# Recurrent solve: two queries of a key in one product, state and query products joined beside copied keys

## The reference, cut to what matters

```
def step(state, inp):
    r_t, w_t, k_t, v_t, a_t, b_t = inp
    sa = einsum('bhij,bhj->bhi', state, a_t)
    state = state * w_t + sa[..., None] * b_t + v_t[..., None] * k_t
    y_t = einsum('bhij,bhj->bhi', state, r_t)
```

## Time and profile before

| | |
|---|---|
| median of 3 runs | 1055.91 us (1055.52 to 1057.32) |
| span of the profiled execution | 1055.6 us |
| PE busy | 1014.7 us (96%), 8574 matmuls |
| DVE busy | 534.4 us (51%) |
| ACT busy | 312.3 us (30%) |
| the recurrent solve | from 199.4 to 319.9 us, 11% of the span |
| mean granted TensorE clock | 0.995 of full |
| HBM read | 272.06 MB |

### The profile page before, as it was taken

One profiled execution on the slowest core, in us unless ns is written; L12 is line 12 of the kernel. 1 busy time (PEld: TensorE's weight loads), 2 busy tenths in 40 slices (PEclk: granted clock), 3 DMA queues, 4 the chain that ended last, 5 costly groups with the idle time before them and its releaser, 6 DMA issues.

```text
span 1055.6 us, 19485 instructions
## 1 busy us (share of the span) xinstructions
PE 1014.7 (96%) x8574; PEld 659.2 (62%) x8574; DVE 534.4 (51%) x815; ACT 312.3 (30%) x536; POOL 131.4 (12%) x152
## 2 busy tenths in 40 slices
PE   8999999999898989999999999999999999999998
PEld 6777899998895678778788443344444443444343
DVE  4568842255546876575665433344333333433354
ACT  4467742033236751231333121111111111111110
POOL 0000000374974500000000100000000000000000
PEclk9999999999999999999999999999999999999999
DMA  9632021000004057466488899999999999999994
GB/s 389 236 116 112 3 81 43 12 5 5 4 4 161 2 186 270 135 224 227 187 368 330 327 409 419 426 427 427 426 427 427 427 425 427 426 428 418 415 415 161
DMA packets 42981, 273.34 MB, mean 259 GB/s; under 512 B 8032, under 2 KB 8176, under 8 KB 28688
## 3 DMA queue, kind: packets, MB, share of 16 engines
q1 hardware_dynamic: 39488, 264.42, 62.1%
q0 software_dynamic: 2400, 4.28, 1.2%
q10 hardware_dynamic: 1008, 3.38, 0.9%
HBM read 272.06 MB, written 4.19 MB: 262 GB/s over the span
## 4 chain that ended last, share of the span: by engine, by line
PE 82%; DMA 8%; DVE 6%; ACT 2%; issue 1%; SPq 0%; DVEq 0%; POOLq 0%; ACTq 0%
PE banks L1722 29%; PE banks L2251 18%; PE banks L2265 9%; DMA w_qkv<-in_w 4%; DMA w_tok<-in_w 4%; PE banks L2289 2%; PE banks L1881 2%; PE banks L2290 2%; PE banks L2257 2%; PE banks L1883 2%; PE banks L1896 1%; PE banks L2237 1%; ACT xT L929 1%; DVE ring L1342 1%; PE banks L1946 1%
## 5 line engine op out<-in xcount | busy, mean ns | idle before, releaser
L1601 DVE TENSOR_TENSOR hid<-banks,silu_a 64x512 f32<-64x512 f32 x32 | 22.2, 693 | 197.9 <-ACT silu_a L934 197.9
L2265 PE MATMUL banks<-w_ring,hidT 128*64 128x512 f32 x512 | 116.8, 598 | 1.1 <-ACT hidT L938 1.1
L1588 DVE SCALAR_TENSOR_TENSOR mod<-banks,row_weight,mod 64x512 f32<-64x512 f32 x64 | 47.9, 748 | 70.3 <-PE banks L2265 69.3
L2251 PE MATMUL banks<-w_tok,xT 128*64 128x512 f32 x176 | 78.3, 596 | 1.8 <-DMA w_ring<-in_w 1.8
L934 ACT ACTIVATE silu_a<-banks 64x512 f32<-64x512 f32 x32 | 18.9, 591 | 206.4 <-PE banks L2252 206.4
L2252 PE MATMUL banks<-w_tok,xT 128*64 128x512 f32 x176 | 79.6, 606 | 0.0
L2252 PE MATMUL banks<-w_ring,xT 128*64 128x512 f32 x176 | 78.3, 596 | 0.0
L1595 DVE TENSOR_TENSOR x<-x,banks 128x1024 f32<-128x1024 f32 x60 | 71.8, 1219 | 12.6 <-PE banks L2290 12.2
L2265 PEld LDWEIGHTS banks<-w_ring,hidT 128*64 128x64 f32 x512 | 34.3, 136 | 67.0 <-issue 65.7
L2251 PE MATMUL banks<-w_ab,xT 128*64 128x512 f32 x160 | 72.4, 606 | 3.8 <-DMA w_tok<-in_w 3.8
L1722 PE MATMUL banks<-x_r,ring_r 128*128 128x512 f32 x192 | 74.8, 390 | 0.0
(11 more groups left out here) (392 smaller groups left out, 2301.6 us busy)
## 6 DMA issues: line engine op xcount, KB each, us to landing
w_ring<-in_w SPq DMA_DIRECT2D x42, 2048.0 KB, 25.5
w_tok<-in_w SPq DMA_DIRECT2D x16, 2048.0 KB, 26.2
ada_buf<-in_w_ada SPq DMA_DIRECT2D x64, 256.0 KB, 3.6
w_ab<-in_w SPq DMA_DIRECT2D x8, 2048.0 KB, 25.9
w_qkv<-in_w SPq DMA_DIRECT2D x7, 2048.0 KB, 29.6
w_tok<-in_w SPq DMA_DIRECT2D x24, 512.0 KB, 16.6
w_ring<-in_w SPq DMA_DIRECT2D x24, 512.0 KB, 17.1
w_ring<-in_w SPq DMA_DIRECT2D x10, 1024.0 KB, 14.6
```

The source lines that it names most:

```text
L1588: dve.scalar_tensor_tensor(dst[:, 512 * n:512 * n + 512], bank[5][SLOTS * n:SLOTS * n + SLOTS, :], weight_of(e), gate2[:, n, :], ALU.mult, ...
L1601: dve.tensor_tensor(hid[:, :], bank[3][SLOTS:P, :], silu_a[:, :], ALU.mult).then_inc(hid_v, 1)
L2251: pe.matmul(bank[2][0:SLOTS, :], rows, w1_of(k), start=(k == 0), stop=(k == KT - 1))
L2265: mm = pe.matmul(bank[5][SLOTS * n:SLOTS * n + SLOTS, :], hidT[:, k, :], w2[:, k, 512 * n:512 * n + 512], start=(k == 0), stop=(k == 3))
```

## The change

- `zr` and `ahat` become two parts of one buffer, so that the two queries of a token, 14 tiles apart, can be read by one product. The addresses stay the same.
- `forms` makes one product of 128 columns per key (the `a` query and the `r` query) where it made two of 64. The order of the forms in `FORMS[k]` turns round: (b, r), (k, r), (b, a), (k, a). The mask follows it.
- `FORMS[k]` gets a fifth form, `BT`: a copy of the keys `Bt`, made by ACT (`end_keys`, one of 128x256 per group and half, before its "x" copies). The group's other buffers move up by 256 floats.
- "gh" multiplies `w_` by (b, r) and by the copied keys in one product of 128 columns. The event "q" on PE is gone, and with it its waits; the query part now lies in the left half of `a_`, the state part in the right half. `queries_added` waits for "gh".

The core of the diff:

```diff
-        FORMS = [flat[:, 3072 * k:3072 * k + 1024].rearrange("p (f h n) -> p f h n", f=4, h=4) for k in range(NG)]
+        FORMS = [flat[:, 3072 * k:3072 * k + 1280].rearrange("p (f h n) -> p f h n", f=5, h=4) for k in range(NG)]
+        RB, KR, TT_, AK, BT = range(5)
...
-        MM_EVENTS = ["ab", "t0", "x"] + LEVELS + ["wu", "gh", "q"]
+        MM_EVENTS = ["ab", "t0", "x"] + LEVELS + ["wu", "gh"]
...
+            def end_keys(half, k):
+                sc, g = 2 * half + k // 2, k % 2
+                act.activation(FORMS[k][:, BT, :, :].rearrange("p (j o) n -> p j o n", o=2),
+                               tokm[:, sc, 2 * g:2 * g + 2, 1, :].rearrange("p j (o n) -> p j o n", o=2), ACT.Copy).then_inc(solve_a[k], 1)
+
+            act.wait_ge(turn_a, TT * CT)
             for half in range(2):
-                for ev in A_EVENTS:
+                for k in range(NG):
+                    end_keys(half, k)
+                for ev in A_EVENTS[1:]:
...
             def queries_added(half, k):
-                dve.wait_ge(solve_mm[k], mm_at(half, "q"))
+                dve.wait_ge(solve_mm[k], mm_at(half, "gh"))
...
-                    for f in range(4):
+                    for f in range(2):
                         for odd, c in ((0, 0), (1, 1), (0, 1), (1, 0)):
-                            key = (bhat[rows, ct, toks], zr[rows, 4 + ct, toks])[f % 2]
-                            query = (ahat[rows, ct, toks], zr[rows, ct, toks])[f // 2]
-                            mm = pe.matmul(bank[2 * k + odd][CH * c:CH * c + CH, P * f + CH * j:P * f + CH * j + CH], key, query, start=True, stop=True)
+                            key = (bhat[rows, ct, toks], zr[rows, 4 + ct, toks])[f]
+                            onto = bank[2 * k + odd][CH * c:CH * c + CH, :].rearrange("p (q f n) -> p q f n", q=2, f=2)[:, :, f, CH * j:CH * j + CH]
+                            mm = pe.matmul(onto, key, zr_all[rows, ct:ct + 15:14, toks], start=True, stop=True)
...
-                        elif ev == "gh":
-                            mm = pe.matmul(a_[rows, at], w_, Bt, start=True, stop=True)
                         else:
-                            mm = pe.matmul(a_[rows, 256 + CH * i:256 + CH * i + CH], w_, rb, start=True, stop=True)
+                            pe.matmul(a_[rows, :].rearrange("p (q h n) -> p q h n", q=2, h=4)[:, :, i, :], w_, FORMS[k][rows, RB:BT + 1:BT, i, :], start=True, stop=True)
...
-                        elif ev == "gh":
-                            pe.wait_ge(solve_a[k], a_at(half, "wu"))
                         else:
-                            pe.wait_ge(solve_v[k], v_at(half, "g"))
+                            pe.wait_ge(solve_a[k], a_at(half, "wu"))
```

More of the change, by code:

```diff
@@ L46, in shape_constants @@
              "before": (r < c) * 1.0,
-             "causal2": np.concatenate([r % CH < np.arange(CH)[None, :], r % CH <= np.arange(CH)[None, :]], 1) * 1.0}
+             "causal2": np.concatenate([r % CH <= np.arange(CH)[None, :], r % CH < np.arange(CH)[None, :]], 1) * 1.0}
     row, col = r % CH, np.arange(CH)[None, :]
@@ L130, in hybrid_layer @@
         hT = sb("hT", [P, KT, SEQ])
-        zr = sb("zr", [P, 14, SEQ])
-        ahat = sb("ahat", [P, CT, SEQ])
+        zr_all = sb("zr", [P, 14 + CT, SEQ])
+        zr, ahat = zr_all[:, 0:14, :], zr_all[:, 14:14 + CT, :]
         bhat = sb("bhat", [P, CT, SEQ])
@@ L765, in _ @@
                         else:
[L766 removed]
+                            src, dst = a_[:, :], group_part(k, 1280, 512, 8)
                         act.activation(dst.rearrange("p h n -> p (h n)"), src, ACT.Copy).then_inc(solve_a[k], 1)
@@ L1274, in queries_added @@
                     for odd in range(2):
-                        ins = dve.tensor_tensor(QQ[k][rows, odd::2, :], f4(a_[rows, 256:512])[:, odd::2, :],
+                        ins = dve.tensor_tensor(QQ[k][rows, odd::2, :], f4(a_[rows, 0:256])[:, odd::2, :],
                                                 zr[HD * odd:HD * odd + HD, 2 * g:2 * g + 2, toks], ALU.add)
@@ L1872, in solve_step @@
                         V_, Bt, Kt_, Ah = (tokm[rows, sc, ct, q, hc] for q in range(4))
-                        tt_, ak, rb = (FORMS[k][rows, f, i, :] for f in range(3))
+                        tt_, ak = (FORMS[k][rows, f, i, :] for f in (TT_, AK))
                         inv, invt, pp, xx = (m[k][rows, i, :] for m in (INV, INVT, PP, XX))
@@ L1933, in outputs @@
                             i = 2 * j + odd
-                            pe.matmul(dst[odd], WU[k][rows, i, HD:P], FORMS[k][rows, 2, i, :], start=True, stop=False)
+                            pe.matmul(dst[odd], WU[k][rows, i, HD:P], FORMS[k][rows, RB, i, :], start=True, stop=False)
                         for odd in range(2):
                             i = 2 * j + odd
-                            mm = pe.matmul(dst[odd], tokm[rows, sc, ct, 0, HD * odd:HD * odd + HD], FORMS[k][rows, 3, i, :], start=False, stop=(at == 0))
+                            mm = pe.matmul(dst[odd], tokm[rows, sc, ct, 0, HD * odd:HD * odd + HD], FORMS[k][rows, KR, i, :], start=False, stop=(at == 0))
                         if at:
```

18 lines of the change are left out of this document (9 added, 9 removed).

## The result

The changed kernel is slower: 1064.63 us median (1056.87 to 1067.72, 15 runs) against 1055.52 us (1052.21 to 1058.58, 15 runs), a ratio of 1.0075 with a 95% interval of 1.0059 to 1.0091. The forecast, 1055.6 with a range up to 1058.2, was wrong. The profiled execution has a span of 1062.9 us, 7.3 more than before, and a mean granted clock of 0.981 where it was 0.995.

The account below looks back on a forecast made before the run. PE bounds the kernel, 82% of the wait chain. Terms -1.55 (first half, interleaved part), +0.1 (end), +1.2 (clock), 0 (forms, "gh", copies) make -0.25 us; with 1055.6 + 0.3, about 1055.6, range up to 1058.2 (own range 1054.2 to 1057.0).

Parts of the forecast that it names:

- Forms: Solve's forms: eight 128-column matmuls per quarter replace sixteen of 64; nothing saved, at most 0.09 us lost per group.
- the line through the earlier trace: Matmul cost fitted through 64 and 512 columns: 0.869 ns a column, 2.7 ns a matmul, so 113.9 ns at 128.
- The overhead rule: Faster rival: 25 ns fixed cost per matmul, forms save 0.2 us a group, 1.4 us in all, 1054.2; chance 0.05.
- "gh" with the query part: In "gh", joined `w_` products need 228 ns a head, fitting under 233; 0.93 us a group stays, cost 0.
- The slower rival, uncovered wide matmuls: Exposed weight loads make wide matmuls 163 ns: 3.0 us in "gh", 2.6 in forms, 1061 in all; chance 0.07.
- "q" gone: First half: `queries_added` no longer waits 0.86 us for "q", so `chain` starts 0.86 us earlier, at 252.4.
- The holes: PE's instruction-packet waits: both interleaved ones (0.69, 0.95 us) go; one of about 1.0 us forms inside the second "gh".
- Copies of the keys: Eight ACT copies of about 0.45 us, before its "x" copies, hidden in ACT's idle time with 3.8 us to spare.
- The clock: PE idle 2.8 us before the first `chain`, then 1.2 GHz: cost 1.2 us; no new fall or hole, chance 0.20.
- The 2.2 us before the level stay, and their fall with them: PE's existing idle time before the second half's doubling level, and the clock fall after it (1.5 us), remain unchanged.
- The second half's end: Packet hole of about 1.0 us inside "gh" delays the last "g"; `chain` can start at 311.8, loss 0.1 us.
- a clock that falls more than once: Slower rival on PE's granted clock, no size given; chance 0.02.

Follow-up runs that it names:

- e3_forms_alone: Kernel before with only the forms joined into 128-column products, "gh" and "q" as they were: 1054.88 us, ratio 0.9974 to the kernel before.
- e1_fill: Changed kernel with whole-array filler products between "gh" and `chain`, 9 in the first half, 5 in the second: 1054.38 us, ratio 0.9965 to the kernel before.
- e5_queries_early: Changed kernel with DVE adding the first two groups' queries between the "g" steps, no filler: 1049.99 us, ratio 0.9925 to the kernel before.
- e10_fill_behind: Changed kernel with 12 whole-array filler products behind the second half's second `chain` step, idle times left open: 1062.72 us, ratio 1.0049 to the kernel before.
- e6_shifted: Kernel before with 32 products of 8 columns (128 instructions, half a packet) put in front of the first forms: 1061.48 us, one execution.
- e4_joined_alone: Changed kernel with the forms back in 64-column products, joined "gh", copied keys and missing "q" kept: 1065.02 us, ratio 1.0077 to the kernel before.
- e8_fill_second: Changed kernel with 5 whole-array filler products before the second half's `chain` only: 1058.45 us, ratio 1.0019 to the kernel before.
- e2_fill_small: Changed kernel with 64x64 filler products between "gh" and `chain`, 32 in the first half, 20 in the second: 1052.96 us, ratio 0.9961 to the kernel before.
- e7_fill_first: Changed kernel with 9 whole-array filler products before the first half's `chain` only: 1057.17 us, ratio 1.0009 to the kernel before.

## Why the prediction was wrong, point by point

*Forms.* Right. A step of eight 128-column matmuls, two in each quarter, takes 0.22 us (199.36, 199.58, 199.80), so 110 ns for one; 113.9 was predicted from the line through the earlier trace rows. The product's own cost was right; in the kernel the joined forms were worth 2.8 us (e3_forms_alone, 1.2 to 4.4) where the sum had 0 for them and about 0.7 for the hole that they remove.

*The overhead rule.* Wrong for this product, as weighed. The Trainium skill's fixed cost on every matmul (TensorEngine Tiling (Array Packing), Instruction Overhead) would have made two 64-column matmuls clearly dearer than one of 128; they took 116.6 against 110 ns, 6.6 ns more and not the 25 estimated.

*"gh" with the query part.* Right. It kept 0.93 us a group (248.00 to 248.93). The slower rival, uncovered wide matmuls, did not happen: 163 ns was its price, 110 was measured in the forms, and "gh" did not get longer.

*"q" gone.* Right in kind. `queries_added` has no idle time before it. `chain` came 1.73 us earlier, where 0.86 was predicted. Of the rest, 0.33 is no merit of the change within the solve: its first forms started at 199.09 instead of 199.42.

*The holes.* Right in place, mostly. Both holes of the interleaved part are gone; the changed kernel ran it at half clock, but e1_fill and e5_queries_early have none there at full clock either. The one expected inside the second "gh" is there, but small: the last "g" waited 0.82 us instead of 0.51, 0.3 us where 1.0 was predicted. Its size is not fixed: in e10_fill_behind, the same program up to there, that "g" waited 1.75 us, 1.2 more. e6_shifted shows that the holes follow the count.

*Copies of the keys.* Right. Four copies at 198.94 take 1.32 us, and ACT then idles 13.72 us before its "x" copies.

```profile
198.94 1.32 ACT L752 ACTIVATE ring<-tokm 128x256 f32<-128x256 f32 x4
...
213.99 1.78 ACT L776 ACTIVATE ring<-banks 128x256 f32<-128x256 f32 x4 [13.72 <-PE banks L1888]
```

*The clock.* This is the step that failed: "I take it that the clock falls here too. The full price is 1.5 us, the lower bound 0 ... I take 1.2." The place and the idle time (2.62 us against 2.8 predicted) were right. The price was carried over from a fall of 3.3 us to a place where the low clock lasted much longer, 13.64 us. Worked out from the starts, the stretch from `chain` to the level lost 4.6 us where a gain of 0.69 (the hole that stood there) had been expected: about 5.3 us for the clock. As a cross-check, the 13.64 and 3.40 us at half clock are at most 8.5 us of PE's work. "The 2.2 us before the level stay, and their fall with them" was wrong too: the idle time and the fall moved in front of the level, into this stretch, and the stage behind the level got 1.2 back. So the clock cost 4.1 us net in this half, not 1.2. How long the first low stretch lasts is not fixed either: behind 2.6 to 2.8 us of idle time it was 13.6 us here and 6.8 us in e4_joined_alone, e8_fill_second and e10_fill_behind.

*The second half's end.* The sum had the hole, the last "g" and the queries, and no clock. PE idled 1.62 us before this `chain` too; 17 us at 1.2 GHz followed 0.9 us later, and the stretch to `row_max` grew by 7.7 us. This term was missing altogether, and it is the largest. The prediction gave 0.02 to "a clock that falls more than once".

The terms as measured in the traced execution: -1.73 (`chain`), -0.69 (hole), +5.3 (clock, the moved fall with it), -1.2 (no fall behind the level), -1.0 (second half's end without its "q"), +7.7 (clock), -1.0 (won back later), 7.4 in sum against 7.3 in the span. Without the two clock terms the change wins, and e1_fill, e2_fill_small and e5_queries_early show that it does.

## What to carry to other kernels

Before work is taken out from between two dependent steps of PE, see what PE does in its place; if it stands still, and thin or waiting work follows, price the clock over all of that work, as a range, and not by one fall seen elsewhere. Cure the idle time by moving up what the next step waits for (here 0.75% under the kernel before), or fill it (0.35 to 0.39%). Joining products that share a weight saves instructions, not columns: next to nothing per product (6.6 ns), and 0.26% of this kernel. That it pays where PE runs through its instructions faster than they come is argued from the holes and not shown by a run.

## What the hardware did that was not expected

- An idle time of PE of 1.6 to 2.6 us was followed by 13.6 and 17.0 us at 1.2 GHz in which PE's row reads 100% busy. The Trainium skill (TensorE: Matmul & The Clock Gate, Part 1: The HAM clock gate) gives the clock back once PE is busy for a while; the traces differ here for `chain` and `outputs`, whose products use a quarter or half of the array, and agree where 12 whole-array products are put in, after 6.8 us in all.
- The same idle time is not always followed by the low clock. Before the level, 2.21 us were followed by it in the kernel before, and 2.22 us were not in e4_joined_alone:

```profile
276.10 0.33 PE L1892 MATMUL banks<-ring 64*64 64x64 f32 x4 [2.22 <-DVE ring L1301]
...
276.10:290.00 13.90, 13.90 (x476) 13.90 (x478) 4.24 (x11) 5.96 (x10) 13.04 (x14) 1.00 0.01 4
```

- By their mean clocks, six runs of twelve of e7_fill_first had a long low stretch. The changed kernel's own runs spread accordingly: three of 1056.9 to 1057.2 us at mean clocks of 0.990 to 0.992, seven of 1064.8 to 1067.7 at 0.980 to 0.982, and five between. How long PE has to stand still for it was not measured.
- Small products keep the clock in front of `chain` (e2_fill_small) and do not restore it behind (the 17.00 us stretch). How dense they have to be was not measured either. In e6_shifted the clock fell for 6.8 us while products of 8 columns ran, without an idle time over 0.69 us before: an idle time is not the only thing that a fall can follow.
- PE's holes without a releaser sit at fixed instruction counts: 128 instructions inserted in front moved two of them by exactly 64 matmuls and their loads. Their size varies from one execution to the next.
